# Down projection of a hybrid attention block: Strassen's scheme in 22 of 44 weight-pair steps in place of 16, its weight sums formed by GpSimd

## The reference

```
h = RMSNorm(x);  p = h @ w_in
r = retention(p[:, :4096]);  s = sliding-window attention(p[:, 4096:])
x = x + concat([r, s]) @ w_out
u = RMSNorm(x) @ w_ffn_in;  a, b = split(u)          # 2 x 5632 columns
g = gelu(causal_conv3(a)) * b
x = x + g @ w_ffn_out                                # 5632 x 2048, the down projection
y = RMSNorm(x)
```

## Time and profile before

| what | value |
|---|---|
| median of 3 runs | 1096.86 us (1096.59 to 1097.03) |
| the profiled execution, its own time | 1096.55 us |
| its span, first to last instruction | 1094.7 us |
| mean granted TensorE clock | 0.998 of full speed |
| TensorE busy with matmuls | 1083.8 us, 99% |
| VectorE, ScalarE, GpSimd busy | 774.4, 586.0, 72.6 us |
| down stage, first to last start of a matmul | 855.86 to 1085.62 us |

### The profile page before, as it was taken

One profiled execution on the slowest core, in us unless ns is written; L12 is line 12 of the kernel. 1 busy time (PEld: TensorE's weight loads), 2 busy tenths in 40 slices (PEclk: granted clock), 3 DMA queues, 4 the chain that ended last, 5 costly groups with the idle time before them and its releaser, 6 DMA issues.

```text
span 1094.7 us, 16468 instructions
## 1 busy us (share of the span) xinstructions
PE 1083.8 (99%) x5751; PEld 922.2 (84%) x5751; DVE 774.4 (71%) x1064; ACT 586.0 (54%) x790; POOL 72.6 (7%) x85
## 2 busy tenths in 40 slices
PE   9999999999999999999999999999999999999996
PEld 7888888888888888888888888888888888888885
DVE  6656776666655665665666657566568999989997
ACT  7445555555555454544545545445455666665663
POOL 2000111111000010101101001011010100000000
PEclk9999999999999999999999999999999999999999
DMA  9866555555566666666666666666666555755741
GB/s 342 282 182 183 159 169 153 165 168 165 168 185 185 176 181 195 188 189 189 192 189 185 186 189 190 191 190 185 186 189 191 172 202 187 248 182 182 258 165 77
DMA packets 146455, 206.84 MB, mean 189 GB/s; under 512 B 7555, under 2 KB 76001, under 8 KB 146160
## 3 DMA queue, kind: packets, MB, share of 16 engines
q1 hardware_dynamic: 145552, 204.17, 61.7%
q0 software_dynamic: 544, 1.69, 0.4%
q10 hardware_dynamic: 320, 0.47, 0.1%
HBM read 204.14 MB, written 2.10 MB: 188 GB/s over the span
## 4 chain that ended last, share of the span: by engine, by line
PE 98%; DVE 1%; DMA 0%; issue 0%; ACT 0%; DVEq 0%; ACTq 0%
PE acc L731 15%; PE acc L480 14%; PE acc L482 13%; PE acc L481 13%; PE acc L739 8%; PE bank_tr L731 7%; PE bank_s L731 7%; PE bank_tr L739 4%; PE bank_s L739 4%; PE bank_s L480 2%; PE bank_s L482 2%; PE bank_s L481 2%; PE bank_tr L481 2%; PE bank_tr L480 2%; PE bank_tr L482 2%; PE bank_s L613 0%
## 5 line engine op out<-in xcount | busy, mean ns | idle before, releaser
L1132 DVE TENSOR_TENSOR w_lo<-raw,w_hi 128x1024 fp32r<-128x1024 f32 x292 | 357.8, 1226 | 269.2 <-ACT w_hi L855 266.5
L855 ACT ACTIVATE w_hi<-raw 128x1024 fp32r<-128x1024 f32 x292 | 309.9, 1062 | 405.2 <-PE acc L482 162.0
L731 PE MATMUL acc<-h_both,w_hi 128*128 128x512 f32 x704 | 218.5, 392 | 0.0
L731 PEld LDWEIGHTS acc<-h_both,w_hi 128*128 128x128 f32 x704 | 126.5, 189 | 21.4 <-DVE rstd_row L1483 0.2
L739 PE MATMUL acc<-h_both,w_lo 128*128 128x256 f32 x704 | 141.4, 282 | 0.0
L480 PE MATMUL acc<-w_hi,h_both 128*128 128x512 f32 (+1 forms) x352 | 137.1, 390 | 0.7 <-DVE h_both L1146 0.7
L482 PE MATMUL acc<-w_hi,h_both 128*128 128x512 f32 (+1 forms) x352 | 133.9, 380 | 0.0
L481 PE MATMUL acc<-w_lo,h_both 128*128 128x512 f32 (+1 forms) x352 | 133.8, 380 | 0.0
L739 PEld LDWEIGHTS acc<-h_both,w_lo 128*128 128x128 f32 x704 | 115.4, 191 | 6.9
L731 PE MATMUL bank_tr<-h_both,w_hi 128*128 128x512 f32 x352 | 108.7, 390 | 0.0
L731 PE MATMUL bank_s<-h_both,w_hi 128*128 128x512 f32 x352 | 108.7, 390 | 0.0
(11 more groups left out here) (258 smaller groups left out, 1646.1 us busy)
## 6 DMA issues: line engine op xcount, KB each, us to landing
raw<-in_w_ffn_in SPq DMA_DIRECT2D x176, 512.0 KB, 3.6
raw<-in_w_ffn_out SPq DMA_DIRECT2D x88, 512.0 KB, 4.3
raw<-in_w_in SPq DMA_DIRECT2D x130, 256.0 KB, 3.0
raw<-in_w_out SPq DMA_DIRECT2D x32, 512.0 KB, 3.9
raw<-in_w_in SPq DMA_DIRECT2D x19, 512.0 KB, 9.7
x_res<-in_x SPq DMA_DIRECT2D x3, 512.0 KB, 8.3
decay<-table_decay POOLq DMA_DIRECT2D x1, 1024.0 KB, 8.8
lnf_row<-in_ln_f SPq DMA_DIRECT2D x1, 1024.0 KB, 7.5
```

The lines of the kernel that those rows point to most:

```text
L731: ins = mm(banks[ft // 2][:, ft % 2, :], w_hi[:, slot, q * COLS + ft * P:q * COLS + (ft + 1) * P], h_both[:, 2 * k + q, :, :].rearrange("p ...
L855: run(w_hi[:, n % SPLIT, :], raw[:, n % RAW, :], ACT.Copy).then_inc(hi_ready, 1)
L1132: tt(w_lo[:, n % SPLIT, :], raw[:, n % RAW, :], w_hi[:, n % SPLIT, :].bitcast(F32), ALU.subtract).then_inc(lo_ready, 1)
```

## The change

- `S_PAIRS` becomes 3, 4, 6, 7, 9, 10, 12, 13, 15, 16, 18 of each sweep: eleven pairs in place of eight.
- The weight sums move from VectorE to GpSimd, in the same four instructions per pair. `t_sum` and `t_hi` become rings of two; `t_lo` lies over `t_sum`, so GpSimd starts the sums of a seven when the seven two before it is used, and the first two sets when the last g is ready.
- For a pair of seven, ScalarE rounds g of the next pair between w_hi and t_hi; VectorE takes the lo part of that g between w_lo and t_lo.
- g's sums are made in eight instructions in place of four, since the pairs no longer lie at one distance.
- The product of the first 1024 columns with the last gain moves from VectorE, at pair 40, to GpSimd, behind all of its sums.

The core of the diff:

```diff
-S_PAIRS = list(range(3, 18, 2))
+S_PAIRS = sorted([*range(3, 19, 3), *range(4, 17, 3)])
+S_SETS = [S_PAIRS[0::2], S_PAIRS[1::2]]
-S_SUMS = 4
+S_SUMS = 4 * len(S_SETS)
+S_RING = 2
...
+            def t_round(r):
+                k = sevens_before(r)
+                own = k % S_RING
+                if k >= S_RING:
+                    act.wait_ge(tile_used, DOWN_TILE + 2 * (seven_at(k - S_RING) + 1))
+                act.wait_ge(t_sum_ready, 4 * k + 4)
+                run(t_hi[:, own], t_sum[:, own], ACT.Copy).then_inc(t_hi_ready, 1)
...
             for r in range(2, LAST_PAIR + 1):
-                g_round(r)
+                if r == 2 or not is_seven(r - 1):
+                    g_round(r)
                 hi_pair(r)
+                if is_seven(r):
+                    g_round(r + 1)
+                    t_round(r)
...
             for r in range(2, LAST_PAIR + 1):
-                g_rest(r)
-                if r < LAST_PAIR and is_seven(r + 1):
-                    weight_sums(r + 1)
+                if r == 2 or not is_seven(r - 1):
+                    g_rest(r)
                 lo_pair(r)
+                if is_seven(r):
+                    g_rest(r + 1)
+                    t_rest(r)
...
+            def weight_sums(r):
+                k = sevens_before(r)
+                own, both = k % S_RING, pair_raw(r)
+                b11, b12 = both[:, 0, 0:COLS], both[:, 0, COLS:2 * COLS]
+                b21, b22 = both[:, 1, 0:COLS], both[:, 1, COLS:2 * COLS]
+                for n in (DOWN_TILE + 2 * r, DOWN_TILE + 2 * r + 1):
+                    pool.wait_ge(raw_landed[n % RAW], landed_value(n))
+                if k < S_RING:
+                    pool.wait_ge(g_ready, 2 * GROUPS)
+                else:
+                    pool.wait_ge(tile_used, DOWN_TILE + 2 * (seven_at(k - S_RING) + 1))
+                combine = nc.gpsimd.tensor_tensor
+                combine(t_sum[:, own, 0, :], b22, b12, ALU.subtract).then_inc(t_sum_ready, 1)
+                combine(b12, b12, b11, ALU.subtract).then_inc(t_sum_ready, 1)
+                pool.wait_ge(t_sum_ready, 4 * k + 2)
+                combine(t_sum[:, own, 1, :], b22, b12, ALU.subtract).then_inc(t_sum_ready, 1)
+                pool.wait_ge(t_sum_ready, 4 * k + 3)
+                combine(t_sum[:, own, 2, :], b21, t_sum[:, own, 1, :], ALU.subtract).then_inc(t_sum_ready, 1)
...
+            for k in range(2 * len(S_PAIRS)):
+                weight_sums(seven_at(k))
+            pool.wait_ge(lnf_landed, 16)
+            pool.wait_ge(g_lo_ready, DOWN_PAIRS + D_MODEL * TOK // (2 * SEQ) + 1)
+            for i in range(2 * TOK):
+                c, t = i // TOK, i % TOK
+                own = slice(c * COLS, (c + 1) * COLS)
+                pool.wait_ge(ffn_added, i + 1)
+                nc.gpsimd.tensor_tensor(y_tok[:, t, own], x_res[:, t, own], lnf_row[:, own],
+                                        ALU.mult).then_inc(first_scaled, 1)
```

More of the change, by code:

```diff
@@ L114, in sevens_before, with seven_at @@
     return sum(is_seven(p) for p in range(pair))
+def seven_at(k):
+    return DOWN_PAIRS * (k // len(S_PAIRS)) + S_PAIRS[k % len(S_PAIRS)]
 def is_head_tile(n):
@@ L210, in build @@
         w_lo_third = sb("w_lo_third", [P, 2, 2 * COLS], F32R)
-        t_hi = sb("t_hi", [P, 3, COLS], F32R)
-        t_lo = sb("t_lo", [P, 3, COLS], F32R)
+        t_hi = sb("t_hi", [P, S_RING, 3, COLS], F32R)
         last_squares = sb("last_squares", [P, 2, SEQ])
-        under_h = sb("under_h", [P, COLS])
+        u_sum = sb("u_sum", [P, COLS])
         over_g = ctx.enter_context(ExitStack())
@@ L220, in build @@
         g_tok = sb("g_tok", [P, FFT, SEQ])
-        g_hi = sb("g_hi", [P, 2, 8, P], F32R)
-        g_lo = sb("g_lo", [P, 2, 8, P], F32R)
+        g_hi = sb("g_hi", [P, 2, S_BLOCKS, P], F32R)
+        g_lo = sb("g_lo", [P, 2, S_BLOCKS, P], F32R)
         over_sums = ctx.enter_context(ExitStack())
-        t_sum = sb("t_sum", [P, 3, COLS], scope=over_sums)
-        u_sum = sb("u_sum", [P, COLS], scope=over_sums)
+        t_sum = sb("t_sum", [P, S_RING, 3, COLS], scope=over_sums)
+        over_sums.close()
+        t_lo = sb("t_lo", [P, S_RING, 3, COLS], F32R, scope=over_sums)
         over_sums.close()
@@ L778, in seven_products @@
                 left, right = slice(0, COLS), slice(COLS, 2 * COLS)
+                own = sevens_before(r) % S_RING
                 def product(out, block, rhs_hi, rhs_lo, starts, stops):
@@ L789, in seven_products @@
                 pe.wait_ge(t_lo_ready, sevens_before(r) + 1)
-                product(others[1][:, 1, :], 5, t_hi[:, 0, :], t_lo[:, 0, :], first, last)
-                product(others[1][:, 0, :], 4, t_hi[:, 1, :], t_lo[:, 1, :], first, last)
-                product(banks[0][:, 1, :], 3, t_hi[:, 2, :], t_lo[:, 2, :], False, False).then_inc(tile_used, 2)
+                product(others[1][:, 1, :], 5, t_hi[:, own, 0, :], t_lo[:, own, 0, :], first, last)
+                product(others[1][:, 0, :], 4, t_hi[:, own, 1, :], t_lo[:, own, 1, :], first, last)
+                product(banks[0][:, 1, :], 3, t_hi[:, own, 2, :], t_lo[:, own, 2, :], False, False).then_inc(tile_used, 2)
             def down_pair(r, banks, others):
@@ L1438, in g_rest, with token_sums @@
                 ins.then_inc(g_lo_ready, 1)
[L1440 to L1444, removed]
+            def token_sums(k, half):
+                pairs, slots = S_SETS[half], slice(half, len(S_PAIRS), 2)
+                step = 2 * (pairs[1] - pairs[0])
+                at = slice(2 * pairs[0], 2 * pairs[-1] + 1, step), slice(2 * pairs[0] + 1, 2 * pairs[-1] + 2, step)
                 g11, g21 = g_tok[:, at[0], 0:P], g_tok[:, at[0], P:SEQ]
                 g12, g22 = g_tok[:, at[1], 0:P], g_tok[:, at[1], P:SEQ]
-                s2, s3, s4 = (g_sums[:, :, i, :] for i in range(3))
+                s2, s3, s4 = (g_sums[:, slots, i, :] for i in range(3))
                 if k == 0:
@@ L1450, in token_sums @@
                 else:
-                    dve.wait_ge(g_sums_ready, k)
+                    dve.wait_ge(g_sums_ready, 2 * k + half - 1)
                 out, in0, in1, op = ((s3, g11, g21, ALU.subtract), (g21, g21, g22, ALU.add),
@@ L1495, in _ @@
                 gate_b(GROUPS - 1, half)
[L1497 to L1514, removed]
             def lo_pair(r):
@@ L1518, in lo_pair, with t_rest @@
                 tt(pair_lo(r), pair_raw(r), pair_hi(r).bitcast(F32), ALU.subtract).then_inc(lo_ready, 2)
-                if is_seven(r):
-                    dve.wait_ge(t_hi_ready, sevens_before(r) + 1)
-                    tt(t_lo[:], t_sum[:], t_hi[:].bitcast(F32), ALU.subtract).then_inc(t_lo_ready, 1)
+            def t_rest(r):
+                own = sevens_before(r) % S_RING
+                dve.wait_ge(t_hi_ready, sevens_before(r) + 1)
+                tt(t_lo[:, own], t_sum[:, own], t_hi[:, own].bitcast(F32),
+                   ALU.subtract).then_inc(t_lo_ready, 1)
             def others_out(sweep):
@@ L1570, in _ @@
                         add_out(i // TOK, i % TOK, a_banks)
[L1571 to L1574, removed]
             dve.wait_ge(x_added, 2 * X_ADDS)
+            dve.wait_ge(lnf_landed, 16)
             for i, (c, t) in enumerate(LAST_BANKS):
@@ L1583, in _ @@
             dve.wait_ge(rstd_ready, 4)
-            dve.wait_ge(scaled, TOK * BLOCKS)
+            dve.wait_ge(first_scaled, 2 * TOK)
+            dve.wait_ge(scaled, 2 * TOK)
             for part in Y_PARTS1[0:2]:
```

22 lines of the change are left out of this document (10 added, 12 removed).

## The result

The changed kernel takes 1155.17 us (median of 4 runs, 1154.8 to 1155.52) against 1096.72 us for the kernel before, timed beside it: 1.0533 times the time, 95% interval 1.0514 to 1.0551. It is **58.5 us slower**. The forecast was 1150.4 us, range 1139 to 1168: the way and the mechanism were right, the sum was 4.8 us short.

A forecast was written before the change was run, and what follows sets the result against it. TensorE's matmuls were taken to bound the down stage, VectorE second. To the profiled 1096.55 us came -4.1 for matmuls, +32.0 for sweep one and +25.6 for sweep two: 1150.1, taken as 1150.4, range 1139 to 1168.

The forecast's parts named there:

- The turns: Down stage: VectorE and GpSimd exclude each other on SBUF, 1.15 us per sum, 21.4 us per triple of pairs.
- The matmuls: Down stage: six more pairs with seven products save 18 matmuls at 0.2267 us, -4.1 us on the path.
- What bounds the kernel before: Down stage before the change: TensorE's matmuls bound it, kept only by 2.4 us of issue; VectorE second.
- Sweep one: Down stage, pairs 3 to 17: five triples each 6.4 us longer than their matmuls, +32.0 us.
- Sweep two: Down stage, second sweep: first triple free because two sets are done ahead, four triples at 6.4 us, +25.6 us.
- the four gain products: On GpSimd under pairs 41 to 43: 4 x 1.15 us, put at about nothing; uncovered up to 4.6.
- A: Rival: VectorE and GpSimd don't exclude each other for these sums, so the kernel is faster, 1092.5 us; chance 0.04.
- B: Rival: TensorE's stalls make the clock fall too, a third of matmuls at 1.2 GHz, about 1195 us; chance 0.05.
- C: Rival: turns mostly hidden by backlog or by VectorE being let through first, half the excess, 1122 us; chance 0.06.
- The order: Down stage: rounding g ahead of t_hi takes 0.6 to 1.1 us of otherwise idle ScalarE, put at about nothing.

The follow-up runs named there:

- e3: Changed kernel with each of GpSimd's 88 sums replaced by a zero fill that writes SBUF and reads nothing: 1091.38 us, ratio 0.995.
- e5: Changed kernel with each GpSimd sum replaced by three fills in a row, making its chain of waits longer: 1094.85 us, ratio 0.9981.
- e9: Changed kernel with each GpSimd sum replaced by a copy of one 128x512 block, one SBUF input instead of two: 1101.48 us, ratio 1.0041.
- e7: Kernel before with the changed order alone (g of the next pair ahead of t_hi and t_lo), sums on VectorE: 1100.24 us, ratio 1.0031.
- e11: Kernel before with the third sum formed as t_sum0 + b11 and the fourth placed behind w_lo of the pair before: 1095.32 us, ratio 0.9982.
- e10: Changed kernel with GpSimd's four gain products replaced by fills of their destination, the product left out, sums kept: 1151.59 us.
- e4: Changed kernel with GpSimd's four gain products made to wait until the last t_lo is ready: 1155.17 us, no change.

## Why the prediction was right, point by point

**The turns** were the step that decided, and they hold: 1.09 us per turn (1.15 less 0.06 forecast), 21.46 us per triple (21.4). e3 and e5 take the reads away and the loss is gone; e9 shortens them, and the loss over a triple's matmuls shrinks from 6.5 to 1.0 us, which is what 12.66 + 8 x 0.41 less 14.96 gives.

**The matmuls**: 18 less at 0.2267 us. e3 shows -5.4, that is the 4.1 and about the 1.5 us that TensorE stood before.

**What bounds the kernel before** was misread in part. I took the 2.4 us of "issue" for nothing; they are TensorE's waits for w_lo, and VectorE set the pace of the first sweep (e7, e11). The forecast hardly felt it, since VectorE in turns is the bound afterwards; it is the 1.5 us of standing that the sum of the parts below takes off.

**Sweep one**: the first matmul with a bank of pair 22 on bank_tr starts at 1001.31 and is the fourth of the pair, so the pair starts at 1000.63. Without stalls 495 matmuls from 855.86 end at 968.1: +32.5 us for a forecast of +32.0. The agreement is partly luck. The five triples give 31.3, and pair 18, the eleventh seven of the sweep, which the sum had forgotten, gives the other 1.3.

**Sweep two** is the step that was mis-sized: +25.6 forecast. From 1000.63, 494 x 0.2267 = 112.0 us would start the last matmul at 1112.6; it starts at 1144.15, +31.5. The last matmuls of pairs 26, 38 and 40 show where it arises:

```profile
1026.24 0.39 PE L490 MATMUL acc<-t_hi,g_lo_third 128*128 128x512 f32 x1
...
1113.28 0.40 PE L490 MATMUL acc<-t_hi,g_lo_third 128*128 128x512 f32 x1
...
1127.62 0.40 PE L490 MATMUL acc<-t_hi,g_lo 128*128 128x512 f32 x1
```

Up to pair 26 are 114 matmuls, which end exactly where they would without a stall (1000.63 + 113 x 0.2267 = 1026.25): the first triple was free, as forecast. GpSimd made both its sets in time, though it could begin the first only at 1000.87, after 24 us of idling:

```profile
1000.87 1.30 POOL L1658 TENSOR_TENSOR t_sum<-raw 128x512 f32<-128x512 f32 x1 [24.18 <-issue]
```

The four triples up to pair 38 take 87.04 us for 264 matmuls, 27.2 too many for 25.6 forecast. A triple without a fall of the clock is 6.5 us too long by itself, and two of the four stretches of low clock lie here; the runs don't part the rest. From pair 38 to pair 40 are 14.34 us for 45 matmuls, which need 10.20: **4.1 us that the sum put at nothing**, and 0.2 come behind them. Most of it is the four gain products, which I had costed at nothing "under pairs 41 to 43": with fills in their place (e10) the same stretch takes 10.72 us, 1124.16 - 1113.44, and the kernel 3.6 less. I weighed them against TensorE's matmuls and not against the engine that is the bound, where no place is free (e4).

The parts add up: -4.1 + 32.5 + 31.5 less the 1.5 us of standing that were there before are 58.4, measured 58.5.

**Rivals.** A (no exclusion) is refuted. Its number, 1092.5, is about what e3 gave (1091.4) once GpSimd read nothing. The Trainium skill (Advanced Engine Details and Errata, VectorE Performance Modes) names in that section only two-port vector instructions for this; the trace differs, with 1.09 us for each fp32 tensor_tensor beside a sum, and the measurement decides. B (the clock) happened in small, and its sign came true, a granted clock below 1.00 before 1140 us: it fell to 0.50 for four stretches of 3.4 us. Each began about a microsecond behind a pause of 2.9 us in which TensorE waited for t_lo, as at 941 to 943 us here; four other such pauses were not followed by one:

```profile
941.00:943.00 2.00, 0.00 (x0) 0.00 (x0) 2.00 (x1) 1.21 (x2) 0.92 (x1) 1.00 0.43 162
...
945.00:947.00 2.00, 2.00 (x6) 1.62 (x5) 2.00 (x3) 0.39 (x2) 0.00 (x0) 0.50 0.11 20
```

Matmuls then start 0.43 us apart, eight in a stretch: 4 x 8 x 0.2 = 6.4 us of TensorE. It fell under the turns: between the last matmuls of every second seven lie 22.2 us next to this stretch (924.09 to 946.25) and 20.2 behind it (to 966.48), 21.2 on average, no more than elsewhere. My evidence against B, that stalls of 3 us were too short, did not hold; that its cost would lie under the turns did. No run took the falls away. C (half of it hidden) is refuted by the period.

**The order** I had costed at nothing for the changed kernel. On the kernel before it costs 3.5 us (e7); on the changed one alone it wasn't tried.

## What to carry to other kernels

Before work goes from VectorE to GpSimd, look in the trace for a place where both run: if the end of one engine's instruction stands a fixed time behind the end of the other's, add their times instead of laying them side by side, and compare the sum with the bound. Then ask what the move saves on the shared time: here a sum cost 0.66 us on VectorE and 1.09 us of VectorE's time on GpSimd, so no dose of it could win. Two engines within 2% of each other are both to be counted as the bound, stage by stage and at the end of the kernel, with every pitch between neighbours that wait for each other. Short pauses that a view lists as "issue" can be waits for the other one.

## What the runs showed that I had not expected

- A fill by GpSimd (write only) beside VectorE costs it nothing (w_lo 2.30 us), a copy with one input costs 0.41 us, a sum with two 1.09 us.
- The clock fell to half for 3.4 us at a time, each time behind a pause of 2.9 us, where I had taken 4 us of idling at 1.00 at the end for a sign that it would not.
- Putting g_lo ahead of t_lo cost 3.5 us, since the instruction that had covered a wait of VectorE was moved away.
- The kernel before was already bound by VectorE in its first sweep: taking 0.24 us per seven off it (e11) won 1.7 us.
